# Moving a kernel's SBUF tensors to other offsets from a 64-byte boundary

## The chip, the cores and the metric

The program runs on one core of one Trainium2 chip. The metric is the device time of one launch in microseconds. Three runs of the kernel before gave a median of 2180.43 us, the lowest 2180.04 and the highest 2180.49.

## The reference

Two transformer blocks are computed one behind the other for 512 tokens of width 1024, in float32. The first puts 16 meta tokens ahead (528 tokens); the second works on 512.

```python
def first_block(x, meta_tokens, ...):
    h = concat([meta, x])
    proj = rms_norm(h, g0) @ w_in
    ...
    h = h + rms_norm((sigmoid(g_a) * y_a + sigmoid(g_b) * y_b) @ w_out, g1)
    u = causal_depthwise_conv(rms_norm(h, g2) @ w_up, conv_w, conv_b)
    h = h + rms_norm((gelu(u_gate) * u_val) @ w_down, g3)
    return h[:, N_META:]

def second_block(x, ...):
    h = h + 0.5 * swiglu(rms_norm_2(h, ffn1_norm), ffn1_w_in, ffn1_w_out)
    h = h + hybrid_mixer(...)
    h = h + 0.5 * swiglu(rms_norm_2(h, ffn2_norm), ffn2_w_in, ffn2_w_out)
    h = h + sigmoid(rms_norm_2(h, ple_norm) @ ple_w_gate) * (p @ ple_w_proj)
    return rms_norm_2(h, final_norm)
```

The attention of the first block (forgetting and stick-breaking heads) and the mixer of the second (chunked linear attention and sparse attention) stand in the program too. The bulk of the work is the product of tokens and weight matrices.

## The kernel before, in words

**Weights in units.** All weights come as one stream of units of 128 x 2048 float32 (1 MB each). A unit `u` lands in `raw[u % 2]` (SyncE's queue). ScalarE rounds it to `whi[u % 2]` in one copy of 2048 columns (`weights_hi`, L766 to L771; a few units in pieces, L783 and L793). GpSimd computes `wlo[u % 2] = raw - whi` in pieces of 512 columns, in a few units of 256 or 128 (`low_part`, L702 to L705). SyncE may fill `raw` again when GpSimd is done with it, and ScalarE may write `whi` again when TensorE is through with the unit two before (`unit_done`).

**Three products for one.** The tokens too are kept as a rounded part and a low part: `xhi` and `xlo` in block 1 (8 rows of 528 or 514 tokens, at a stride of 576), `x2hi` and `x2lo` in block 2 (8 rows of 512), `hhi` and `hlo` for the inner rows of the feed-forward layers (22 rows of 512). `tile_products` (L2362 to L2369) takes a weight tile of 128 columns (512 bytes per partition) as the stationary operand and makes three products with it: `whi` with the rounded tokens, `whi` with the low ones, `wlo` with the rounded ones. The tokens are the moving operand:

```python
for p_, (w, xx) in enumerate(((whi, xh), (whi, xl), (wlo, xh))):
    for dst, tok in places:
        ins = mm(dst, w[slot][:, cols], xx(tok), ...)
```

In block 2 one matmul streams 512 tokens. In block 1 a row of 514 or 528 tokens goes as two matmuls, 256 and 258 (or 272). Every matmul has a weight load of its own (an LDWEIGHTS in the trace, engine name PEld). In the trace a matmul is written `ps<-moving,stationary`.

**Places in SBUF.** Everything is placed by hand. `at(name, shape, dtype, offset)` (L223 to L228) puts a tensor at a byte offset in each partition, or at the next free one. The program begins at 16512, and in the kernel before this is how the large ones stand:

| tensor | offset before | modulo 64 | modulo 256 |
|---|---|---|---|
| raw0, raw1 | 16512, 24704 | 0 | 128 |
| whi0, whi1 | 32896, 41088 | 0 | 128 |
| wlo0, wlo1 | 49280, 57472 | 0 | 128 |
| h | 65664 | 0 | 128 |
| xhi (x2hi), xlo | 82560, 100992 | 0 | 128 |
| x2lo | 98944 | 0 | 128 |
| arena (hhi) | 119424 | 0 | 128 |
| hlo | 164480 | 0 | 128 |
| ident | 209536 | 0 | 128 |
| temp | 213408 | 32 | 160 |

"arena" is the shared region: the attention's tensors, the mixer's, `hhi` and `hlo`, the tensors of squares and the output rows all lie in it, nearly all of them at multiples of 64 bytes from its start. "temp" is the scratch region behind the constants, and its tensors start at 32 modulo 64 in the main (`dl`, `dpt`, `sb_lo`, `ntri_r`, `sb_p`, `nt`).

Not everything that TensorE reads starts on the boundary even so. Block 1 leaves the first 14 tokens out from its gates on (`SKIP = 14`): `wide_places(banks, 14)` makes the moving operand start at token 14 of a row, 56 bytes past a boundary, and its second part at token 270, likewise 56 bytes past one. The up projection of block 1 takes rows of 514 tokens from token 0 (`places_of`), on the boundary. `L2592` turns `fox_p` (in arena, on the boundary) with `ident`, and `L3187` turns `dl` (in temp, 32 bytes past one) with `ident`; in both the tile that is turned is the stationary operand. `L3177` streams `dpt` (temp, 32 past) against `ckvt` (arena, 0), `L3104` streams `kx` against `kx` (arena, 0 and 0), and `L2669` streams `sb_hi` (arena, 0) and then `sb_lo` (temp, 32 past) against `ntri_r` (temp, 32 past).

**Order of the work.** Each engine's program is written out by hand, with semaphores between the engines. No planner or scheduler reads the offsets.

Of the kernel before, what the change touches and what calls it, by code (L numbers as in the profile page):

```python
# [25 lines left out]
F32R = mybir.dt.float32r  # L26
# [5 lines left out]
P = 128  # L32
D = 1024
KC = D // P
META = 16
SEQ = 512
# [5 lines left out]
HALF = 256  # L42
XROW = 576
BANK = 512
FF = 2816
FC = FF // P
EPS = 1e-6
NEG = -1e30
UT = 16
# [66 lines left out]
def std_units(w, starts):  # L116

    tiles = w.reshape(KC, P, w.shape[1])
    cut = [tiles[:, :, s:s + P] for s in starts]
    both = [np.stack(cut[i:i + 2]) for i in range(0, len(cut), 2)]  # L120
    return [np.ascontiguousarray(b.transpose(2, 1, 0, 3)).reshape(1, P, UT * P) for b in both]


def row_units(w, start):

    tiles = w[:, start:start + BANK].reshape(2, KC // 2, P, BANK)
    return [np.ascontiguousarray(t.transpose(1, 0, 2)).reshape(1, P, UT * P) for t in tiles]
# [18 lines left out]
def pairs_up(w):  # L146
    starts = []
    for i in range(0, FC, 2):
        starts += [P * i, P * i + P, FF + P * i, FF + P * i + P]
    return std_units(w, starts)  # L150
# [6 lines left out]
def layout(v):  # L157
# [15 lines left out]
    narrow = [w[:, 4112:4240], w[:, 4752:4824], decay, np.zeros((D, 8), np.float32), decay, decay]  # L173
    aw = np.zeros((P, BANK), np.float32)
    stacked = np.zeros((P, 2), np.float32)
# [33 lines left out]
def build(nc, wstream, h0, fw, cvec, alpha_w, rel_bias, p2, ident_c, masks_c, gmask_c, onehot_c, out):  # L209
    n_units = wstream.shape[0]  # L210
    with ExitStack() as ctx:
# [9 lines left out]
        place = {"at": 16512}  # L221

        def at(name, shape, dt=F32, offset=None):  # L223
            size = int(np.prod(shape[1:])) * 4
            if offset is None:
                offset = place["at"]
                place["at"] += (size + 31) // 32 * 32
            return nc.alloc_sbuf_tensor_at(name, list(shape), dt, offset=offset)  # L228

        raw = [at(f"raw{b}", [P, UT * P]) for b in range(2)]  # L230
        whi = [at(f"whi{b}", [P, UT * P], F32R) for b in range(2)]
        wlo = [at(f"wlo{b}", [P, UT * P], F32R) for b in range(2)]
        h = at("h", [P, KC, T1])
        x_at = place["at"]
        xhi, xlo = (at(name, [P, KC, XROW], F32R)[:, :, 0:T1] for name in ("xhi", "xlo"))
        x_spare = x_at + 8 * KC * SEQ
        arena = place["at"]
        place["at"] += 2 * FC * SEQ * 4
        ident = at("ident", [P, P])
        masks_at = place["at"]  # L240
        masks = at("masks", [P, 3 * P + META])
# [21 lines left out]

        ps = ctx.enter_context(nc.psum_tensor("ps", [P, 8 * BANK], F32))
        regions = ps[:].rearrange("p (r c) -> p r c", c=2 * BANK)
        LO = BANK - HALF

# [3 lines left out]
        def bank(i, n=1):  # L271
            return ps[:, i * BANK:(i + n) * BANK]

# [50 lines left out]
        yt = [at(f"yt{i}", [P, TN], offset=temp + 4 * T1 * i) for i in range(4)]  # L324
        mix = at("mix", [P, KC, SEQ], offset=x_at)
        x2hi = at("x2hi", [P, KC, SEQ], F32R, offset=x_at)
        x2lo = at("x2lo", [P, KC, SEQ], F32R, offset=x_at + 4 * KC * SEQ)

        sq = [at(f"sq{i}", [P, T1], offset=temp + 4 * T1 * i) for i in range(2)]
        nt = [at(f"nt{i}", [P, T1], offset=temp + 4 * T1 * (2 + i)) for i in range(3)]  # L330
# [9 lines left out]
            return sq_sum1[:] if T == TN else sq_sum[:, 0:T]  # L340

        hhi = at("hhi", [P, FC, SEQ], F32R, offset=arena)
        hlo = at("hlo", [P, FC, SEQ], F32R, offset=arena + 4 * FC * SEQ)
        cg = at("cg", [P, 2, SEQ], offset=temp)
        gact = at("gact", [P, 2, SEQ], offset=temp + 4096)
        cvl = at("cvl", [P, 2, SEQ], offset=temp + 8224)
# [2961 lines left out]
```

How the kernel before makes its waits and increments, by code:

```python
    def wait(self, value=None):  # L104
        self.eng.wait_ge(self.sem, self.turn + (self.n if value is None else value))
# [571 lines left out]
        @block.sync  # L677
        def _(sp):
            sp.dma_start(cv[:], cvec).then_inc(sig("gains_in"), 16)
            for q in range(4):
                sp.dma_start(h[:, 2 * q:2 * q + 2, :], h0[:, 2 * q:2 * q + 2, :]).then_inc(sig(f"h_in{q}"), 16)
            sp.dma_start(raw[1][:], wstream[1]).then_inc(sig("raw_ready1"), 16)
            with sp.Fori(1, n_units // 2) as i:
                for b in range(2):
                    sp.wait_ge(sig("lo_done"), i * 2 + (b - 1))
                    sp.dma_start(raw[b][:], wstream[bass.ds(i * 2 + b, 1)].rearrange("u p n -> (u p) n")
                                 ).then_inc(sig(f"raw_ready{b}"), 16)
            if n_units % 2:
                sp.wait_ge(sig("lo_done"), n_units - 2)
                sp.dma_start(raw[0][:], wstream[n_units - 1]).then_inc(sig("raw_ready0"), 16)
            for j, half in [(j + e, half) for j in (0, 2) for half in range(2) for e in range(2)]:
                cols = slice(half * BANK, (half + 1) * BANK)
                sp.wait_ge(sig("out_odd" if j % 2 else "out_even"), 2 * (j // 2) + half + 1)
                sp.dma_start(out[0, j * P:(j + 1) * P, cols], outb[j][:, cols]).then_inc(sig("stored"), 16)
            sp.wait_ge(sig("stored"), 128)
# [207 lines left out]
            def fox_hi(m):  # L905
                act.wait_ge(sig("o_done"), m + 2)
                if m == 0:
```

## Time and profile before

| | |
|---|---|
| median of 3 runs | 2180.43 us |
| the profiled execution's own time | 2180.01 us |
| its span in the trace | 2178.2 us |
| TensorE matmuls busy | 2146.8 us (99%), x12490 |
| TensorE weight loads busy | 1851.4 us (85%), x12490 |
| VectorE busy | 995.2 us (46%) |
| ScalarE busy | 755.5 us (35%) |
| GpSimd busy | 1008.7 us (46%) |
| DMA | 195.17 MB, mean 90 GB/s |

The span is the stretch from the first to the last instruction, and the execution's time lies 1.8 us above it. Busy times of an engine are unions of its instructions' spans. Matmuls overlap one another in the trace (each lasts longer than the step from one start to the next), so the pace is read from starts: from a timeline, or from the number of matmuls in a stretch that has no gap.

### The profile page before, as it was taken

The page shows a single profiled execution, that of the slowest core. Times are in us where ns is not written, and L with a number is a line of the kernel's source. Part 1 is how long each engine was busy: PE and PEld are TensorE (multiplying, and loading weights), DVE is VectorE, ACT ScalarE, POOL GpSimd, SP SyncE. Part 2 cuts the span into 40 slices and gives each one's busy share as a digit, 9 for nine tenths or more (in the row PEclk, how much of TensorE's full clock was granted, in tenths as well). Part 3 has the DMA queues.
Part 4 walks back from the last instruction along what each step waited for, and adds up shares of the span by engine and source line. Part 5 has one row for each costly group of instructions (what it writes and reads, how often), then busy time and mean ns, then how long its engine had stood idle before and what let it go on. Part 6 is the DMA issues. An engine that isn't in the chain of part 4 may idle for free.

```text
span 2178.2 us, 31347 instructions
## 1 busy us (share of the span) xinstructions
PE 2146.8 (99%) x12490; PEld 1851.4 (85%) x12490; DVE 995.2 (46%) x1460; ACT 755.5 (35%) x1017; POOL 1008.7 (46%) x825
## 2 busy tenths in 40 slices
PE   8999999999999999999999999999999999999998
PEld 7897999999999887888888788878788888888886
DVE  5144454379888207322200819671876442222027
ACT  4133455243222215322211415551336332222134
POOL 4322223455555547555544545254331555555444
PEclk9999999999999999999999999999999999999999
DMA  4311111212222222322222221114220222222222
GB/s 165 102 69 68 59 48 71 97 59 97 96 83 90 106 96 106 127 96 96 97 97 96 93 109 42 59 58 152 80 78 21 97 97 97 96 96 97 96 100 93
DMA packets 31950, 195.17 MB, mean 90 GB/s; under 512 B 3968, under 2 KB 4480, under 8 KB 10096
## 3 DMA queue, kind: packets, MB, share of 16 engines
q1 hardware_dynamic: 26352, 182.66, 23.1%
q10 hardware_dynamic: 5504, 11.18, 1.6%
q8 instruction: 68, 1.11, 0.2%
q14 instruction: 26, 0.21, 0.0%
HBM read 189.47 MB, written 4.23 MB: 89 GB/s over the span
## 4 chain that ended last, share of the span: by engine, by line
PE 83%; issue 7%; DVE 5%; POOL 3%; ACT 1%; DMA 0%; SPq 0%; DVEq 0%; POOLq 0%; ACTq 0%
PE ps L2367 73%; POOL wlo L705 3%; PE ps L2962 2%; DVE sqa L1517 1%; PE ps L3177 1%; PE ps L3161 1%; PE ps L3044 1%; DVE x2lo L1505 1%; PE ps L3097 1%; PE ps L2646 1%; PE ps L2669 0%; PE ps L3142 0%; PE ps L2705 0%; PE ps L3187 0%; DMA h<-h 0%
## 5 line engine op out<-in xcount | busy, mean ns | idle before, releaser
L705 POOL TENSOR_TENSOR wlo<-raw,whi 128x512 fp32r<-128x512 f32 (+2 forms) x820 | 1007.3, 1261 | 1143.8 <-ACT whi L771 1037.9
L771 ACT CAST whi<-raw 128x2048 fp32r<-128x2048 f32 x162 | 309.6, 1911 | 811.8 <-PE ps L2367 754.5
L2367 PE MATMUL ps<-x2hi,whi 128*128 128x512 f32 x1136 | 448.6, 395 | 1.2 <-DVE x2lo L1505 1.1
L2367 PE MATMUL ps<-x2hi,wlo 128*128 128x512 f32 x1136 | 442.4, 389 | 0.0
L2367 PE MATMUL ps<-x2lo,whi 128*128 128x512 f32 x1136 | 442.1, 389 | 0.0
L2367 PE MATMUL ps<-xhi,whi 128*128 128x256 f32 (+2 forms) x1336 | 273.3, 286 | 11.7 <-DVE xlo L1571 9.3
L2367 PE MATMUL ps<-xlo,whi 128*128 128x256 f32 (+2 forms) x1336 | 270.7, 284 | 0.0
L2367 PE MATMUL ps<-xhi,wlo 128*128 128x256 f32 (+2 forms) x1336 | 270.5, 284 | 0.0
L2367 PEld LDWEIGHTS ps<-x2hi,whi 128*128 128x128 f32 x1136 | 213.3, 188 | 49.7 <-issue 4.8
L2367 PEld LDWEIGHTS ps<-x2hi,wlo 128*128 128x128 f32 x1136 | 213.2, 188 | 44.7
L2367 PEld LDWEIGHTS ps<-x2lo,whi 128*128 128x128 f32 x1136 | 213.4, 188 | 44.4 <-issue 1.7
L2367 PEld LDWEIGHTS ps<-xhi,whi 128*128 128x128 f32 x1336 | 208.6, 191 | 12.9 <-POOL wlo L705 12.0
L2367 PEld LDWEIGHTS ps<-xlo,whi 128*128 128x128 f32 x1336 | 208.7, 191 | 0.0
L2367 PEld LDWEIGHTS ps<-xhi,wlo 128*128 128x128 f32 x1336 | 208.6, 191 | 0.0
L2367 PE MATMUL ps<-hhi,whi 128*128 (+1 forms) x528 | 205.4, 389 | 0.0
L2367 PE MATMUL ps<-hlo,whi 128*128 (+1 forms) x528 | 205.4, 389 | 0.0
L2367 PE MATMUL ps<-hhi,wlo 128*128 (+1 forms) x528 | 205.4, 389 | 0.0
L2367 PEld LDWEIGHTS ps<-hhi,wlo 128*128 128x128 f32 x528 | 99.1, 188 | 20.8
L2367 PEld LDWEIGHTS ps<-hhi,whi 128*128 128x128 f32 x528 | 99.1, 188 | 20.5
L2367 PEld LDWEIGHTS ps<-hlo,whi 128*128 128x128 f32 x528 | 99.1, 188 | 20.4
L1529 DVE TENSOR_TENSOR cvl<-ps,fold 128x1024 f32<-128x1024 f32 x22 | 26.9, 1224 | 189.3 <-PE ps L2367 189.3
L2002 DVE SCALAR_TENSOR_TENSOR h<-ps,h 128x512 f32<-128x512 f32 x16 | 10.9, 681 | 209.7 <-PE ps L2367 209.7
(471 smaller groups left out, 2761.0 us busy)
## 6 DMA issues: line engine op xcount, KB each, us to landing
raw<-wstream SPq DMA_DIRECT2D x170, 1024.0 KB, 4.8
h<-h SPq DMA_DIRECT2D x4, 528.0 KB, 8.5
ncb<-c_rows ACTq DMA_DIRECT2D x8, 256.0 KB, 3.3
ple_rows<-ple_out ACTq DMA_DIRECT2D x4, 512.0 KB, 4.0
bias<-bias_rows ACTq DMA_DIRECT2D x8, 256.0 KB, 4.8
ple<-ple_rows ACTq DMA_DIRECT2D x4, 512.0 KB, 5.4
out_dram<-outb SPq DMA_DIRECT2D x8, 256.0 KB, 2.9
raw<-wstream ACTq DMA_DIRECT2D x4, 256.0 KB, 7.2
```

The lines of the kernel that those rows point to most:

```text
L705: return nc.gpsimd.tensor_tensor(wlo[b][:, cols], raw[b][:, cols], whi[b][:, cols].bitcast(F32), ALU.subtract)
L771: nc.scalar.copy(whi[b][:], raw[b][:]).then_inc(sig("hi_done"), 1)
L1505: vec.scalar_tensor_tensor(out=xl[:, k, 0:T], in0=view(k), scalar=cv[:, gain + k:gain + k + 1], in1=xh[:, k, 0:T].bitcast(F32), op0=ALU.mu ...
L1517: vec.tensor_tensor(squared[:, 0, :], squared[:, 0, :], squared[:, k, :], ALU.add).then_inc(sig("sq_added"), 1)
L1529: return vec.tensor_tensor(dst, pair(src), scale, ALU.mult)
L2367: ins = mm(dst, w[slot][:, cols], xx(tok), start=first and p_ == 0, stop=last and p_ == 2, skip_group_check=True)
L2646: mm(zs[x][:, col + b * P:col + (b + 1) * P], qkb[rows_of(x), 4 + c, b * P:(b + 1) * P], qkb[rows_of(x), c, i * P:(i + 1) * P], start=(q = ...
L2962: ins = mm(gv_bank(half, j), xx[:, k if first else k + 4, tok], ww[u % 2][:, cols], start=(first and k == 0 and p_ == 0), stop=(not first ...
L3044: ins = mm(bank(5 + e)[:, t_ * P:(t_ + 1) * P], gvt[:, s_, (2 * hd + e) * P:(2 * hd + e + 1) * P], rhs, start=(x_ == 0), stop=(x_ == len(p ...
L3097: ins = mm(dst, left, right, start=True, stop=True)
L3161: mm(dst, dq[:, hd, j * P:(j + 1) * P], ckvf[:, 0:w], start=True, stop=False)
L3177: ins = mm(bank(6 + m % 2)[:, 0:P], ckvt[:, b, :], dpt[m % 2][:, b * P:(b + 1) * P], start=(b == 0), stop=(b == j))
```

## The change

Four things are moved; no instruction is added, removed or put elsewhere. `raw` stays where it is, and so do the order and the shape of every matmul, copy and transfer.

```diff
+SKEW = (0, 32, 64, 128)
...
-        whi = [at(f"whi{b}", [P, UT * P], F32R) for b in range(2)]
-        wlo = [at(f"wlo{b}", [P, UT * P], F32R) for b in range(2)]
+        w_at = place["at"]
+        whi, wlo = ([at(name + str(b), [P, UT * P], F32R, offset=w_at + (2 * i + b) * 4 * UT * P + SKEW[2 * i + b])
+                     for b in range(2)] for i, name in enumerate(("whi", "wlo")))
+        place["at"] = w_at + 4 * (4 * UT * P) + 128
         h = at("h", [P, KC, T1])
         x_at = place["at"]
         xhi, xlo = (at(name, [P, KC, XROW], F32R)[:, :, 0:T1] for name in ("xhi", "xlo"))
-        x_spare = x_at + 8 * KC * SEQ
-        arena = place["at"]
-        place["at"] += 2 * FC * SEQ * 4
+        x_spare = x_at + 8 * KC * SEQ + 32
+        arena = place["at"] + 32
+        place["at"] += 32 + 2 * FC * SEQ * 4 + 32
...
-        x2lo = at("x2lo", [P, KC, SEQ], F32R, offset=x_at + 4 * KC * SEQ)
+        x2lo = at("x2lo", [P, KC * SEQ + 8], F32R, offset=x_at + 4 * KC * SEQ)[:, 4:4 + KC * SEQ].rearrange(
+            "p (k n) -> p k n", n=SEQ)
...
-        hlo = at("hlo", [P, FC, SEQ], F32R, offset=arena + 4 * FC * SEQ)
+        hlo = at("hlo", [P, FC * SEQ + 8], F32R, offset=arena + 4 * FC * SEQ)[:, 4:4 + FC * SEQ].rearrange(
+            "p (k n) -> p k n", n=SEQ)
```

Where the tensors stand with it:

| tensor | offset after | modulo 64, before -> after | modulo 256 after |
|---|---|---|---|
| raw0, raw1 | 16512, 24704 | 0 -> 0 | 128 |
| whi0 | 32896 | 0 -> 0 | 128 |
| whi1 | 41120 | 0 -> 32 | 160 |
| wlo0 | 49344 | 0 -> 0 | 192 |
| wlo1 | 57600 | 0 -> 0 | 0 |
| h | 65792 | 0 -> 0 | 0 |
| xhi (x2hi), xlo | 82688, 101120 | 0 -> 0 | 0 |
| x2lo | 99088 | 0 -> 16 | 16 |
| arena (hhi) | 119584 | 0 -> 32 | 32 |
| hlo | 164656 | 0 -> 48 | 48 |
| ident | 209728 | 0 -> 0 | 64 |
| temp | 213600 | 32 -> 32 | 96 |

## Rows read from the trace of the kernel before

**Rows 1.** The page: busy time, share and instructions of TensorE's matmuls and loads.

```profile
PE 2146.8 (99%) x12490; PEld 1851.4 (85%) x12490; DVE 995.2 (46%) x1460; ACT 755.5 (35%) x1017; POOL 1008.7 (46%) x825
```

**Rows 2.** The page's costliest groups: busy us, mean ns, then idle before and its releaser.

```profile
L2367 PE MATMUL ps<-x2hi,whi 128*128 128x512 f32 x1136 | 448.6, 395 | 1.2 <-DVE x2lo L1505 1.1
L2367 PE MATMUL ps<-x2lo,whi 128*128 128x512 f32 x1136 | 442.1, 389 | 0.0
...
L2367 PE MATMUL ps<-xhi,whi 128*128 128x256 f32 (+2 forms) x1336 | 273.3, 286 | 11.7 <-DVE xlo L1571 9.3
...
L2367 PEld LDWEIGHTS ps<-x2hi,whi 128*128 128x128 f32 x1136 | 213.3, 188 | 49.7 <-issue 4.8
...
L2367 PE MATMUL ps<-hhi,whi 128*128 (+1 forms) x528 | 205.4, 389 | 0.0
L2367 PE MATMUL ps<-hlo,whi 128*128 (+1 forms) x528 | 205.4, 389 | 0.0
```

**Rows 3.** Busy time by stretch: block 2's up projection, down projection, block 1's up projection.

```profile
core 0: us, PE busy (x) PEld busy (x) DVE busy (x) ACT busy (x) POOL busy (x), PEclk, DMA share, GB/s
900.00:1050.00 150.00, 150.00 (x664) 124.20 (x663) 40.40 (x28) 40.85 (x28) 78.48 (x56) 1.00 0.26 97
1100.00:1160.00 60.00, 60.00 (x267) 49.67 (x266) 0.00 (x0) 9.54 (x5) 29.30 (x24) 1.00 0.24 89
500.00:650.00 150.00, 150.00 (x1250) 149.80 (x1249) 132.24 (x115) 38.78 (x27) 82.24 (x53) 1.00 0.25 91
```

**Rows 4.** Timeline of TensorE, block 1, moving operand from token 0: start us, length us.

```profile
600.08 0.40 PE L2367 MATMUL ps<-xhi,wlo 128*128 128x256 f32 x2
...
601.28 0.28 PE L2367 MATMUL ps<-xlo,whi 128*128 128x256 f32 x1
```

**Rows 5.** Timeline of TensorE, block 1, moving operand from token 14.

```profile
218.55 0.40 PE L2367 MATMUL ps<-xlo,whi 128*128 128x256 f32 x2
...
220.71 0.28 PE L2367 MATMUL ps<-xlo,whi 128*128 128x256 f32 x1
```

**Rows 6.** Lines L2592, L3187, L3177 and L3104: duration ns min/median/max.

```profile
L2592 PEld LDWEIGHTS ps<-ident,fox_p x80: 138/141/144, 111.8 to 232.6; 128*128 128x128 f32 x80
L2592 PE MATMUL ps<-ident,fox_p x80: 272/273/328, 111.9 to 232.7; 128*128 128x128 f32 x80
...
L3187 PEld LDWEIGHTS ps<-ident,dl x80: 137/141/146, 1624.9 to 1671.0; 128*128 128x128 f32 x80
L3187 PE MATMUL ps<-ident,dl x80: 272/273/332, 1625.2 to 1671.1; 128*128 128x128 f32 x80
...
L3177 PE MATMUL ps<-dpt,ckvt x160: 270/275/347, 1627.1 to 1672.3; 128*128 128x128 f32 x160
...
L3104 PE MATMUL ps<-kx,kx x16: 275/275/275, 1344.4 to 1403.4; 128*128 128x128 f32 x16
```

**Rows 7.** Groups of TensorE by shape: the matmul with both operands 32 past.

```profile
L2669 PE MATMUL ps<-sb_lo,ntri_r 128*128 128x512 f32 x20 | 7.9, 394 | 0.0
```

**Rows 8.** Timeline of GpSimd, block 2's up projection; in brackets its idle time before.

```profile
957.71 6.32 POOL L705 TENSOR_TENSOR wlo<-raw,whi 128x512 fp32r<-128x512 f32 x4 [5.89 <-ACT whi L771]
968.53 5.04 POOL L705 TENSOR_TENSOR wlo<-raw,whi 128x512 fp32r<-128x512 f32 x4 [4.50 <-ACT whi L771]
```

**Rows 9.** Line L771, duration as above, and groups of ScalarE by shape.

```profile
L771 ACT CAST whi<-raw x162: 1888/1912/1941, 15.6 to 2142.7; 128x2048 fp32r<-128x2048 f32 x162
...
L1001 ACT CAST sb_hi<-sb_p 128x512 fp32r<-128x512 f32 x20 | 12.1, 623 | 9.4 <-DVE sb_p L1778 9.4
L783 ACT CAST whi<-raw 128x512 fp32r<-128x512 f32 x20 | 11.9, 607 | 0.0
```

## The prediction
> **What bounds the kernel now.** I read the page first. TensorE's matmuls cover 2146.8 us of a span of 2178.2 [rows 1], so all idle time of TensorE together is 31.4 us. VectorE, ScalarE and GpSimd are busy for less than half of the span. So the kernel can get shorter or longer by more than a per cent only if the step from one matmul to the next changes, or if another engine gets so much slower that TensorE has to wait for it.
>
> The costliest groups came next [rows 2]. Nearly all of TensorE's time lies in one line, L2367, the three products. Block 2 has 1136 matmuls of each of three kinds with 512 moving columns, the three feed-forward down projections 528 of each of three kinds, block 1 three times 1336 of some 257 columns. Their mean durations (389 ns, 286 ns) are no pace, since they overlap. The pace comes from stretches without a gap [rows 3]: 664 matmuls touch 150 us of block 2's up projection, two of which only reach over the edges, so 150 us / 662 = 226.6 ns a step. The down projection gives 60 us / 265 = 226.4 ns, block 1's up projection 150 us / 1248 = 120.2 ns. The granted clock in all three is 1.00 [rows 3], the upper level of 2.4 GHz. At that clock 512 columns take 213.3 ns and 257 take 107.1 ns. So each step holds 13.3 ns or 13.1 ns beside the stream, and these are about the same for a long stream and for one of half the length. Only this rest could be a matter of where operands lie: 4992 x 13.3 ns + 4008 x 13.1 ns = 66.4 + 52.5 = 119 us. The question is whether it is one.
>
> **The change part by part.** Nothing is added or taken out. Of the offsets modulo 64, `whi0`, `wlo0` and `wlo1` do not move at all (their shifts of 0, 64 and 128 bytes are whole multiples of 64), nor do `raw`, `h`, `xhi`, `xlo`, `x2hi`, `ident` and temp. What moves is `whi1` (to 32), `x2lo` (16), `hhi` and everything else in arena (32) and `hlo` (48). I cost four things.
>
> (a) *Moving operands off the boundary*: `x2lo` in 1136 matmuls, `hhi` and `hlo` in 3 x 528 = 1584, together 2720. The trace of before has the same product with a moving operand on the boundary and off it. On it, in block 1's up projection, five pairs of matmuls (256 and 258 columns) take 601.28 - 600.08 = 1.20 us, 240 ns a pair [rows 4]. At token 14, 56 bytes past the boundary in both parts of the pair, nine pairs take 220.71 - 218.55 = 2.16 us, again 240 ns [rows 5]. The difference is nothing, and the timeline's last digit (0.01 us over nine pairs) leaves 1.1 ns a pair, 0.6 ns a matmul, in either direction. A stream of 512 columns crosses twice as many boundaries, so I allow 1.2 ns: 2720 x 1.2 ns = 3.3 us, up or down. I take 0, since both pairs read 240.
>
> This is weighed against a rule. By the Trainium skill ("SBUF — State Buffer", Door 1, on cachelines) an access that crosses into a new line of 16 bytes costs a penalty. All new offsets are multiples of 16, so by that rule none of the moved operands touches a line more, and the term is 0; rows 5, whose start lies 8 bytes past such a line, show no cost even there.
>
> (b) *Stationary operands off the boundary*: loads from `whi1`. It serves every second unit and two of three products, about a third of 12490 loads. The trace has the same load on and off the boundary: `fox_p` lies at 0, `dl` at 32 modulo 64, each is turned with `ident` in 80 matmuls, and their loads last 138/141/144 ns and 137/141/146 ns, their matmuls 272/273 ns both [rows 6]. In block 2 a load lasts 188 ns of a step of 226.6 [rows 2, 3], so 38 ns more would be hidden. In block 1 the loads cover 149.80 of 150 us [rows 3] and could be what sets the step. There a change by the last digit of these durations, 1 ns, on a third of 4008 loads would be 1.3 us. I take 0.
>
> (c) *ScalarE and GpSimd on moved tiles.* The rows give one hint of a price: ScalarE's copy of 512 columns takes 607 ns from a source on the boundary and 623 ns from one 32 bytes past it [rows 9], though the two also differ in what they wait for. Taken at its worst that is 16 ns for 512 columns, 64 ns on the 1912 ns of a unit of `whi1` [rows 9]. No row shows GpSimd with other offsets. What hides both: TensorE works 48 x 226.6 ns = 10.9 us on a unit, and the next unit needs 1.9 us on ScalarE and then 5.0 to 6.3 us on GpSimd [rows 8, 9], 8.2 us at most. So 2.7 us are free, over 40% of GpSimd's work; its idle time of 4.50 and 5.89 us before a unit [rows 8] says the same. Cost 0. If GpSimd took over 40% longer, TensorE would wait at each unit.
>
> (d) *What is on the path between the stages.* All waits of TensorE together are 31.4 us [rows 1]. If every operation that ends one were longer in the proportion 623 to 607 [rows 9], that would be 31.4 x 0.026 = 0.8 us. I take 0 here too.
>
> **Sum.** The profiled execution took 2180.0 us with its span of 2178.2 and 1.8 us around it, and lies 0.4 us under the median of the runs, 2180.4. The change adds 0, with bounds of -3.3 us and +3.3 + 1.3 + 0.8 = +5.4 us. So I forecast **2180.4 us**, with 2177.1 to 2185.8 as this case's own bounds. A measurement of this kernel can tell 0.2%, some 4.4 us, from no change.
>
> **Rivals.**
>
> *The clash goes (faster).* The rest of 13.3 ns a step may be a clash inside SBUF: the stream and the next tile's load read from the same offset modulo 64 at the same time. For it: in before all large operands share the offset 0, and the rest is the same in every group. Where the moving operand is moved, 2720 matmuls, the clash would go: 2720 x 13.3 ns = 36.2 us, **2144.2 us**. It decides from 1.6 ns a matmul (4.4 us / 2720). Against it: rows 5 have moving and stationary operands 56 bytes apart and run at the same 240 ns as rows 4, where they share the offset. A chance of 9%, for offsets like 16 and 48 that no row has, and for lesser gains.
> A page has the same gain from another side. By the Trainium skill ("TensorE: Matmul & The Clock Gate", Back-to-back issue gap) matmuls of 512 columns follow each other in N/2.4 + 2.5 ns, 215.8 ns; by that the trace is 10.8 ns over, and the moved 2720 would give 29.4 us if the offset were the reason. The same page (LDWEIGHTS, Part 2) gives TensorE two independent read ports, for stream and loads, and by that there is no clash to lose.
>
> *Each stream off the boundary pays (slower).* The one matmul of 512 columns with both operands 32 bytes past the boundary, `sb_lo` against `ntri_r`, lasts 394 ns on average [rows 7], against 389 ns for the dense products [rows 2]. If these 5 ns are the price of an offset, it falls on the 2720 matmuls of `x2lo`, `hhi` and `hlo`, in the feed-forward layers and in the mixer's projections: 2720 x 5 ns = 13.6 us, **2194.0 us**. It too decides from 1.6 ns a matmul. Against it: only 20 matmuls, between neighbours of other shapes, which change a modelled end; and rows 4 and 5 again. A chance of 14%, which includes a GpSimd that takes over 40% longer on `whi1`.
>
> *The change does less than it says.* Three of the four shifts of the weight buffers are multiples of 64, so for them nothing could come even if the offset modulo 64 mattered. It gives the forecast's time and is part of its chance.
>
> **How the numbers follow.** No change has 77%, since the two rows that could have shown an effect, one for each operand, show none to within a nanosecond. The faster rival has 9%, the slower one 14%. The range must take in a bit more than the likeliest case: it goes from 2176.5, just under its lower bound, to 2187.0, half the price of the slower rival (2180.4 + 6.8). Left out are the full prices of both rivals.
>
> **What would show it.** Right: `x2lo` and `hlo` products keep 389 ns, 150 us of block 2's up projection hold 664 matmuls or one or two more or fewer, and the down projection's 60 us hold 267; loads from `whi` keep 188 ns; the idle time of TensorE stays near 31 us. The faster rival would show as some 677 matmuls in those 150 us (three steps of 226.6 ns less 13.3) and 283 in those 60; the slower one as some 659 and 261. Steps that differ between odd and even units would tell of `whi1`. New waits of TensorE for GpSimd's L705 at every second unit would say that (c) was wrong. The forecast is wrong if 16 or 48 bytes act otherwise than the 32 and 56 that the rows hold.

## The result and the profile after

The changed kernel is slower: 2212.1 us (median of four runs, 2211.92 to 2212.38), against 2180.2 us for the kernel before on the same chip, a ratio of 1.0147 with a 95% interval from 1.0135 to 1.0159. The forecast was no change, 2180.4 us, in a range from 2176.5 to 2187.0.

The page of the changed kernel, busy time and the groups that answer to those of [rows 2] (L2367 is now L2372):

```profile
span 2210.2 us, 31347 instructions
...
PE 2179.2 (99%) x12490; PEld 1852.8 (84%) x12490; DVE 992.5 (45%) x1460; ACT 756.6 (34%) x1017; POOL 1006.8 (46%) x825
...
L2372 PE MATMUL ps<-x2hi,whi 128*128 128x512 f32 x1136 | 453.9, 400 | 0.8 <-DVE x2lo L1510 0.7
L2372 PE MATMUL ps<-x2hi,wlo 128*128 128x512 f32 x1136 | 449.6, 396 | 0.0
L2372 PE MATMUL ps<-x2lo,whi 128*128 128x512 f32 x1136 | 447.0, 393 | 0.0
L2372 PE MATMUL ps<-xhi,whi 128*128 128x256 f32 (+2 forms) x1336 | 272.7, 285 | 12.6 <-DVE xlo L1576 9.4
...
L2372 PEld LDWEIGHTS ps<-x2hi,whi 128*128 128x128 f32 x1136 | 213.5, 188 | 54.2 <-issue 4.6
...
L2372 PE MATMUL ps<-hhi,wlo 128*128 (+1 forms) x528 | 208.3, 395 | 0.0
L2372 PE MATMUL ps<-hhi,whi 128*128 (+1 forms) x528 | 208.2, 394 | 0.0
L2372 PE MATMUL ps<-hlo,whi 128*128 (+1 forms) x528 | 207.4, 393 | 0.0
```

The number of instructions is the same, and so are the busy times of the other engines to 3 us. TensorE's idle time is 31.0 us (2210.2 - 2179.2), as before (31.4). No wait has come in: the whole loss of 32.0 us in the span is in the matmuls themselves. Every product with 512 columns got longer, by 4 to 7 ns, **also those whose moving operand did not move modulo 64** (`x2hi` with `whi` and `wlo`). The products with 256 to 272 columns and the weight loads kept their means to 1 ns.

The three stretches of [rows 3] in the changed kernel, same columns:

```profile
900.00:1050.00 150.00, 150.00 (x647) 120.99 (x646) 37.66 (x26) 37.91 (x26) 77.65 (x55) 1.00 0.26 91
1100.00:1160.00 60.00, 60.00 (x260) 48.57 (x259) 2.05 (x1) 10.37 (x6) 30.71 (x24) 1.00 0.25 88
500.00:650.00 150.00, 150.00 (x1247) 150.00 (x1246) 131.54 (x115) 38.86 (x27) 81.58 (x53) 1.00 0.26 91
```

With two matmuls over the edges left out, the step in block 2 is 150 us / 645 = 232.6 ns (226.6 before), in the down projection 60 / 258 = 232.6 (226.4), in block 1's up projection 150 / 1245 = 120.5 (120.2). The granted clock is 1.00 in all three, so it has no part in it. The loss adds up step by step: both kernels have the same 12490 matmuls in the same order, so each step from one start to the next can be compared with its like before. The steps of the x2 products grew by 19.1 us in all, those of `hhi` and `hlo` by 8.7, the other products with 512 columns (three sets of 192 in the mixer with other moving tokens, two of 192 with the weights as the moving operand) by 4.4, block 1's by 0.7; steps over 320 ns, which hold the waits, shrank by 1.0. That is 31.9 us.

The timeline of TensorE in the changed kernel, block 2's up projection, start and length in us; between the two rows lie nine rounds of three products:

```profile
900.09 0.39 PE L2372 MATMUL ps<-x2hi,whi 128*128 128x512 f32 x1
...
906.39 0.39 PE L2372 MATMUL ps<-x2hi,whi 128*128 128x512 f32 x1
```

A round takes 6.30 us / 9 = 700 ns, where before it took 680 (three times 226.7). The single steps from start to start in such a round are 229, 234 and 237 ns in one unit, and go through a cycle of nine values between 225 and 238 ns in the next (mean 231.9); before, all were 226 or 227. So the units of both weight buffers are slowed, and not only those of `whi1`.

### The profile page after: what moved, and what is told of

Same layout as the page of the kernel before. It is cut to its first block, busy times and chain, and to the rows that moved or that the text cites. A ratio compares the mean times of both kernels' runs of the same rounds, so it can differ in the third digit from the quotient of the medians.

```text
span 2210.2 us, 31347 instructions
## 1 busy us (share of the span) xinstructions
PE 2179.2 (99%) x12490; PEld 1852.8 (84%) x12490; DVE 992.5 (45%) x1460; ACT 756.6 (34%) x1017; POOL 1006.8 (46%) x825
## 4 chain that ended last, share of the span: by engine, by line
PE 85%; issue 7%; DVE 4%; POOL 3%; ACT 1%; DMA 0%; SPq 0%; DVEq 0%; POOLq 0%; ACTq 0%
PE ps L2372 75%; POOL wlo L710 3%; PE ps L2967 2%; PE ps L3182 1%; PE ps L3166 1%; PE ps L3049 1%; PE ps L3102 1%; PE ps L2651 0%; PE ps L2674 0%; PE ps L3147 0%; PE ps L2710 0%; PE ps L3192 0%; DMA h<-h 0%; DVE sqa L1522 0%; DVE h L1566 0%
## 5 line engine op out<-in xcount | busy, mean ns | idle before, releaser
L710 POOL TENSOR_TENSOR wlo<-raw,whi 128x512 fp32r<-128x512 f32 (+2 forms) x820 | 1005.5, 1259 | 1176.7 <-ACT whi L776 1070.0
L776 ACT CAST whi<-raw 128x2048 fp32r<-128x2048 f32 x162 | 309.6, 1911 | 840.0 <-PE ps L2372 781.5
L2372 PE MATMUL ps<-x2hi,whi 128*128 128x512 f32 x1136 | 453.9, 400 | 0.8 <-DVE x2lo L1510 0.7
L2372 PE MATMUL ps<-x2hi,wlo 128*128 128x512 f32 x1136 | 449.6, 396 | 0.0
L2372 PE MATMUL ps<-x2lo,whi 128*128 128x512 f32 x1136 | 447.0, 393 | 0.0
L2372 PE MATMUL ps<-xhi,whi 128*128 128x256 f32 (+2 forms) x1336 | 272.7, 285 | 12.6 <-DVE xlo L1576 9.4
L2372 PE MATMUL ps<-xhi,wlo 128*128 128x256 f32 (+2 forms) x1336 | 271.4, 285 | 0.0
L2372 PE MATMUL ps<-xlo,whi 128*128 128x256 f32 (+2 forms) x1336 | 270.3, 284 | 0.0
L2372 PEld LDWEIGHTS ps<-x2hi,whi 128*128 128x128 f32 x1136 | 213.5, 188 | 54.2 <-issue 4.6
L2372 PEld LDWEIGHTS ps<-x2lo,whi 128*128 128x128 f32 x1136 | 213.4, 188 | 52.3 <-issue 1.7
L2372 PEld LDWEIGHTS ps<-x2hi,wlo 128*128 128x128 f32 x1136 | 213.2, 188 | 50.6
L2372 PEld LDWEIGHTS ps<-xhi,whi 128*128 128x128 f32 x1336 | 208.5, 190 | 13.8 <-POOL wlo L710 13.1
L2372 PE MATMUL ps<-hhi,wlo 128*128 (+1 forms) x528 | 208.3, 395 | 0.0
L2372 PEld LDWEIGHTS ps<-xhi,wlo 128*128 128x128 f32 x1336 | 208.3, 190 | 0.0
L2372 PE MATMUL ps<-hhi,whi 128*128 (+1 forms) x528 | 208.2, 394 | 0.0
L2372 PEld LDWEIGHTS ps<-xlo,whi 128*128 128x128 f32 x1336 | 208.0, 190 | 0.0
L2372 PE MATMUL ps<-hlo,whi 128*128 (+1 forms) x528 | 207.4, 393 | 0.0
L2372 PEld LDWEIGHTS ps<-hhi,wlo 128*128 128x128 f32 x528 | 99.0, 188 | 23.7
L2372 PEld LDWEIGHTS ps<-hlo,whi 128*128 128x128 f32 x528 | 99.2, 188 | 23.5
L2372 PEld LDWEIGHTS ps<-hhi,whi 128*128 128x128 f32 x528 | 99.3, 188 | 22.9
```

What stands on the lines that cost most here:

```text
L710: return nc.gpsimd.tensor_tensor(wlo[b][:, cols], raw[b][:, cols], whi[b][:, cols].bitcast(F32), ALU.subtract)
L776: nc.scalar.copy(whi[b][:], raw[b][:]).then_inc(sig("hi_done"), 1)
L2372: ins = mm(dst, w[slot][:, cols], xx(tok), start=first and p_ == 0, stop=last and p_ == 2, skip_group_check=True)
```

## The experiments

Two questions: does the 64-byte boundary of an operand count (theory A), or the place of the operands against each other (theory R; the first four expectations call it theory B)? And with what period, and in which direction? The kernel before gives a hint that the prediction overlooked: all large operands of it stand not just on 64-byte boundaries but at the same place modulo 512 (32896, 82560, 98944, 119424 and 164480 all leave 128). "Distance" below is a token operand's offset minus that of the weight tiles. It is given modulo 512, which is the length of a weight tile; the length of a block 2 token row, 2048 bytes, is a multiple of it. Block 1's rows have a stride of 2304 bytes, so there the distance of a row alternates between the one given and 256 bytes more.

Every kernel of this section but the last was run once. The kernel before, in 15 runs, lay between 2179.9 and 2180.8 us, so differences of 12 us and more are far outside its spread. The first four stand beside one run of it at 2179.9 us.

**weights_only.** The weights as in the change, the rest back.

```diff
-        place["at"] = w_at + 4 * (4 * UT * P) + 128
+        place["at"] = w_at + 4 * (4 * UT * P) + 256
...
-        x_spare = x_at + 8 * KC * SEQ + 32
-        arena = place["at"] + 32
+        x_spare = x_at + 8 * KC * SEQ
+        arena = place["at"]
```
(`x2lo` and `hlo` have no shift of their own; all that stands behind the weights is 256 bytes further than in the kernel before)

> The four weight buffers stand as in the changed kernel (whi1 32 bytes past a 64-byte boundary, wlo0 and wlo1 shifted by 64 and 128); x2lo, hhi, hlo and the shared region are back on multiples of 256 bytes from where they stood before. Theory A (each operand off a 64-byte boundary pays by itself, and 2720 moving operands carry most of it): most of the 32 us goes, about 2185 us, and in block 2's up projection only the unit in whi1 has steps above 226.6 ns. Theory B (what counts is where the moving stream lies relative to the load that runs beside it, and before all were alike): the offsets between stream and loads are still changed, so the steps stay near 232 ns in units of both buffers and the time near 2205 to 2212 us. Theory C (placement modulo 128 or 256 bytes counts): as B here.

Measured: 2202.8 us.

**tokens_only.** `SKEW = (0, 0, 0, 0)` and no gap behind the weights; the token side as in the change.

> The weight buffers stand as before; x2lo (+16), the shared region with hhi (+32) and hlo (+48) as in the changed kernel. Theory A: nearly the whole loss, some 2205 us; x2hi steps stay at 226.6 ns and those of x2lo, hhi and hlo grow by 5 to 15 ns. Theory B: a loss as well, but also in steps of x2hi beside which no load has moved only if the order of phases drifts; between 2195 and 2212 us. Both expect the same for odd and even units, since the two buffers are alike again.

Measured: 2206.6 us. Either half of the change alone has most of the whole loss, 23 and 27 of 32 us, so the two halves do not add up.

**all_by_64.** `SKEW = (0, 64, 64, 128)`, shared region and `x2lo` each 64 bytes further.

> Every shift is a multiple of 64 bytes: weights 0, 64, 64, 128, x2lo +64, shared region +64. Theory A and a theory B that counts modulo 64: the time of before, 2180 us, all steps 226.6 ns. Theory C (the offsets modulo 128 or 256 bytes count): a loss of 10 us or more, with steps that differ from 226.6 ns.

Measured: 2212.6 us, the changed kernel's time with every large tensor back on a 64-byte boundary. Theory A falls here.

**low_parts_only.** `x2lo` and `hlo` 16 bytes off, the rest at multiples of 64 bytes from its old place (the shared region at 256).

> Only x2lo and hlo are 16 bytes off; everything else is at multiples of 256 bytes from its place before. Theory A: 1136 + 528 = 1664 matmuls pay, 10 to 20 us, in their own step alone. Theory B: a loss of like size; the step of x2lo or hlo changes and its neighbours may too. If the low parts cost nothing: 2180 us.

Measured: 2205.4 us. The groups of block 2's up projection (900 to 1050 us) show that the products whose operands stand as before pay too. First the kernel before, then this one:

```profile
L2367 PE MATMUL ps<-x2hi,whi 128*128 128x512 f32 x222 | 86.4, 389 | 0.0
L2367 PE MATMUL ps<-x2lo,whi 128*128 128x512 f32 x221 | 86.0, 389 | 0.0
L2367 PE MATMUL ps<-x2hi,wlo 128*128 128x512 f32 x221 | 86.0, 389 | 0.0
```

```profile
L2373 PE MATMUL ps<-x2hi,wlo 128*128 128x512 f32 x216 | 85.5, 396 | 0.0
L2373 PE MATMUL ps<-x2lo,whi 128*128 128x512 f32 x216 | 85.1, 394 | 0.0
L2373 PE MATMUL ps<-x2hi,whi 128*128 128x512 f32 x216 | 84.9, 393 | 0.0
```

The mixer's products with 512 columns whose operands all moved by 256 bytes or not at all (`xr`, `gy`, `my`, 571 steps compared) stayed the same to 0.2 ns a step on average.

**tokens_by_32, tokens_by_64, tokens_by_256.** The whole token side moved as one against the weights, which stand as before.

```diff
-        x_at = place["at"]
+        x_at = place["at"] + 32
+        place["at"] += 32
```

> All token operands (xhi, xlo, x2hi, x2lo, and the shared region with hhi and hlo) are moved together by 32 bytes against the weight buffers, and keep their places relative to each other. Before, every large operand stood at the same place modulo 512 bytes. Theory S (all streams, and all loads, must be alike among themselves): they still are, so 2180 us and steps of 226.6 ns. Theory R (what counts is the distance of the stream from the load beside it): the distance is now 32 for every pair, so all steps of a unit are alike but another value than 226.6, up or down, and both buffers show it; 5 ns a step would be 30 us. Theory A (each operand off a 64-byte boundary): 226.6 ns plus a price in every step.

> The same with 64 bytes. Theory S: 2180 us. Theory R: another value than 226.6 ns in every step, near that of 32 bytes if the effect is smooth. Theory A: 2180 us, since nothing is off a 64-byte boundary.

> The same with 256 bytes. Theory S: 2180 us. Theory R: if the pattern repeats in 256 bytes or less, 226.6 ns and 2180 us; if in 512 (a weight tile is 512 bytes wide, a token row 2048), this is the largest distance there is, and the steps are other than 226.6 ns, by the sum of the first runs some 230 to 235 ns and 2205 to 2215 us, or below 226.6 if the equal places of before are the worst.

Measured, beside 2180.7 us for the kernel before: 2211.7, 2193.1 and 2181.2 us. Block 2's up projection, the stretch 900 to 1050 us of each, in this order:

```profile
900.00:1050.00 150.00, 150.00 (x645) 120.47 (x644) 37.22 (x27) 39.29 (x27) 73.31 (x53) 1.00 0.27 98
```
```profile
900.00:1050.00 150.00, 150.00 (x657) 123.05 (x657) 38.33 (x27) 40.67 (x28) 76.08 (x54) 1.00 0.27 98
```
```profile
900.00:1050.00 150.00, 150.00 (x663) 124.21 (x662) 40.39 (x28) 40.84 (x28) 77.73 (x55) 1.00 0.27 98
```

Steps of 233.3, 229.0 and 226.9 ns. Theory S, that streams need only be alike among themselves, is out: they are alike here, and 32 bytes cost 31 us. 64 bytes, which leave every operand on its boundary, cost 12 us; 256 bytes cost 0.5 us in one run, less than the 0.9 us by which the runs of the kernel before differ. These are means of a round. At 64 bytes the three products of a round have steps of 232 (`x2hi,whi`), 226 (`x2lo,whi`) and 229 ns (`x2hi,wlo`), though all three have the same distance: the distance sets the mean, not each single step.

**dist_16_128_16, dist_48_96_192, dist_96_16_128, dist_8_8_48.** One distance for each set of token operands in one kernel: `xhi`/`xlo` (inside their rows, which have 192 bytes to spare), `x2hi`/`x2lo`, `hhi`/`hlo`. For the first:

```diff
-        xhi, xlo = (at(name, [P, KC, XROW], F32R)[:, :, 0:T1] for name in ("xhi", "xlo"))
+        xhi, xlo = (at(name, [P, KC, XROW], F32R)[:, :, 4:4 + T1] for name in ("xhi", "xlo"))
...
-        x2hi = at("x2hi", [P, KC, SEQ], F32R, offset=x_at)
+        x2hi = at("x2hi", [P, KC * SEQ + 32], F32R, offset=x_at)[:, 32:32 + KC * SEQ].rearrange(
+            "p (k n) -> p k n", n=SEQ)
```
(likewise `x2lo`, `mix` and the small tensors in their place, `hhi` and `hlo`)

> All weight buffers as before. Each pair of token operands (rounded and low part alike) has a distance of its own from the weight tiles: xhi/xlo 16 bytes, x2hi/x2lo 128, hhi/hlo 16 (528). Theory R (a step depends on this distance alone): each group has one mean step of its own; so far 32 bytes gave 233.3 ns, 64 gave 228.9, 256 and 0 gave 226.7. I expect hhi/hlo at 16 above 228 ns, x2 at 128 between 226.7 and 229, falling towards the period. Theory A (each operand's own 64-byte boundary): x2 226.7, hhi/hlo at 233. If the cost grows with the row's place in the region rather than with the distance, none of this holds and groups that share a distance differ.

> The same with 48 bytes for xhi/xlo, 96 for x2hi/x2lo, 192 for hhi/hlo. Theory R with a period of 64 bytes would give 96 the 233.3 ns of 32, which theory A gives as well; with a period of 256 the distance of 192 equals -64 and should be as 64 or mirrored, up to 229 ns. A step below 226.6 ns anywhere would make a faster kernel.

> The same with 96, 16 and 128 bytes. Theory R: x2 at 16 and hhi/hlo at 128 repeat, to 0.3 ns, the means that hhi/hlo at 16 and x2 at 128 have in the kernel before this one. If they do not, the distance alone is not the cause.

> The same with 8, 8 and 48 bytes (560). Theory R, where the unit is a line of 16 bytes: 8 bytes cost little or nothing; where the unit is 64 bytes, 8 and 48 lie with 32 at 230 ns or more. In block 1, where 32 bytes gave 120.1 ns for 121.4, distances under 64 should give some of the same gain.

Measured, beside 2180.2 us: 2202.4, 2212.0, 2209.3 and 2209.7 us. Mean step of TensorE by distance, worked out from the starts in each trace (all steps of the group under 260 ns; block 1 is its up projection, 500 to 700 us, steps under 150 ns of 256 and 258 columns):

| distance, bytes | x2 products, ns | hhi/hlo products, ns | block 1, ns |
|---|---|---|---|
| 0 (before) | 227.0 | 226.7 | 120.0 |
| 8 | 233.0 | | 120.0 |
| 16 | 231.7 | 231.7 | 117.5 |
| 32 | 233.3 | 233.3 | 118.3 |
| 48 | | 233.3 | 116.7 |
| 64 | 229.0 | 228.9 | 118.3 |
| 96 | 233.4 | | 118.9 |
| 128 | 232.9 | 233.0 | |
| 192 | | 233.3 | |
| 256 | 227.0 | 226.7 | 120.0 |

A distance gives the same mean step to two sets of operands in different regions: to 0.1 ns at 16 and 128 (in different kernels), 32 and 64, and to 0.3 ns at 0 and 256. The cost is neither smooth nor mirrored: 64 costs 2.2 ns, 192 costs 6.7. Nothing tried is under 226.7 ns for 512 columns, so the kernel before stood at the best place found, and the slowest step is 233.3 to 233.4 ns: 6.7 ns more, which at 2.4 GHz is the time of 16 columns. The expected repeat of 16 and 128 in the third kernel came, within the 0.3 ns asked for. My expectation that 128 lies near the minimum, between 226.7 and 229, missed; so did those that 192 costs as much as 64, that 8 bytes might cost little, and that every distance under 64 gives block 1 some gain (8 gives none).

Block 1 goes the other way: 0, 8 and 256 are the worst distances of the table. Its streams from token 14 (200 to 350 us) lie 56 bytes further on; there the kernel before (56 bytes) has 120.0 ns, dist_8_8_48 (64) 118.5 and tokens_by_64 (120) 121.0, so block 1 has slower places too. Down projection of the first and the third kernel, for `hhi`/`hlo` at 16 and at 128 (one matmul more or less in 260 is 0.9 ns a step, so these counts are coarser than the table):

```profile
1100.00:1160.00 60.00, 60.00 (x260) 48.70 (x260) 0.00 (x0) 11.45 (x6) 25.91 (x21) 1.00 0.30 105
```
```profile
1100.00:1160.00 60.00, 60.00 (x259) 48.27 (x258) 1.68 (x1) 9.55 (x5) 29.27 (x23) 1.00 0.26 89
```

**together_by_32.** Weights, tokens and shared region all 32 bytes further: `SKEW = (32, 32, 32, 32)`, 32 bytes behind the weights.

> Weight buffers, tokens and shared region all 32 bytes further, so every operand of the large products is off a 64-byte boundary and every distance is 0. Theory R (the distance between stream and weight tiles, modulo 256 bytes, sets the step): 226.7 ns a step for 512 columns and 2180 us, as before. Theory A (an operand's own boundary): 233 ns as with the tokens alone moved by 32 bytes, 2212 us.

Measured: 2181.1 us, beside 2180.5. Every operand of the large products is off its 64-byte boundary, and the stretch of block 2 is that of [rows 3] to one matmul:

```profile
900.00:1050.00 150.00, 150.00 (x663) 124.20 (x662) 40.34 (x28) 40.80 (x28) 77.99 (x55) 1.00 0.28 98
```

So with 512 columns an operand's own boundary costs nothing that these runs can tell, and the distance between tokens and weights carries the loss. `raw` stayed where it was, so the place of tokens and weights against `raw` does not count either.

**wlo_by_32.** Only `wlo0` and `wlo1` moved: `SKEW = (0, 0, 32, 32)`, 256 bytes behind the weights.

> Only wlo0 and wlo1 are moved, by 32 bytes. If a stream is slowed by the load that runs beside it: in block 2's up projection the x2lo product (beside it, wlo is loaded) is slow, some 235 ns or more, and the other two stay near 226.7. If by its distance from its own stationary tile: the x2hi,wlo product is slow. Either way less than the 31 us that all three cost at 32 bytes; a third would be some 10 us, 2190 us, but the patterns of the first runs say that a phase drifts on from one step to the next, so all three may move and the sum may be up to 2205 us.

Measured: 2215.5 us, the slowest of all, where at most 2205 was expected. The groups of block 2's up projection:

```profile
L2373 PE MATMUL ps<-x2lo,whi 128*128 128x512 f32 x215 | 86.0, 400 | 0.0
L2373 PE MATMUL ps<-x2hi,whi 128*128 128x512 f32 x215 | 84.9, 395 | 0.0
L2373 PE MATMUL ps<-x2hi,wlo 128*128 128x512 f32 x215 | 83.6, 389 | 0.0
```

The product that is made with the moved `wlo` kept its 389 ns. The longest is `x2lo,whi`, beside which the moved tile is loaded. That is what a stream held up by the load beside it would show, and not what its own stationary tile would. But `x2hi,whi`, beside which an unmoved tile is loaded, has 395, and the steps from start to start (232 ns for `x2hi,whi`, 239 for `x2lo,whi`, 229 for `x2hi,wlo`) are all over 226.7. So moving one tile changes all steps of a round, and the run does not settle which operands are in each other's way. It does speak against GpSimd, which writes the moved `wlo`: all 214 steps of `x2lo,whi` in the 150 us are 239 ns, while GpSimd is busy for 77.63 of them.

**xhi_by_16.** The version that the table points to: block 2 stays at distance 0, block 1 gets 16. The whole edit to the kernel before:

```diff
-        xhi, xlo = (at(name, [P, KC, XROW], F32R)[:, :, 0:T1] for name in ("xhi", "xlo"))
+        xhi, xlo = (at(name, [P, KC, XROW], F32R)[:, :, 4:4 + T1] for name in ("xhi", "xlo"))
```

> Only xhi and xlo of block 1 are moved, by 16 bytes inside their rows; block 2 keeps its distance of 0. From the stretches of the kernel that had 16 bytes there: 2.5 us less in block 1's up projection, 0.9 in its output projection, some 1.1 in the stretches with attention. Theory R: 2175.5 us, 0.2% less than before. If gains in block 1 are given back as waits for VectorE (88% busy in the up projection) or at the start of block 2: 2178 to 2180.

Measured: 2176.0 us (median of 11 runs) against 2180.5 (15 runs), a ratio of 0.9981, interval 0.9972 to 0.9990. It beats both kernels. Its stretches of block 1 and block 2:

```profile
500.00:650.00 150.00, 148.23 (x1262) 148.03 (x1261) 134.20 (x116) 38.72 (x27) 81.52 (x52) 1.00 0.27 92
900.00:1050.00 150.00, 150.00 (x664) 124.20 (x663) 39.58 (x28) 38.52 (x28) 78.70 (x56) 1.00 0.26 94
```

Between 480 and 710 us TensorE now has a wait that it had not before:

```profile
PE ps L2367 <- POOL wlo L705: 1.8, 1, 1.8
```

Block 2 is unchanged at 664. Block 1's up projection has 2112 products (22 units of 96); at 2.5 ns less each (120.0 to 117.5) they should give 5.3 us. Not all of it is kept: only 12 more matmuls fit into the 150 us, since 1.77 us of them are idle now (150 - 148.23). TensorE waits there, by the profile for GpSimd; GpSimd got its unit from ScalarE, which rounded it (from 541.13 us) right behind a cast of `hhi` for which it had waited 5.15 us for VectorE. A second new wait of 1.7 us, for VectorE (`first_up`, L1869), lies at 476 us. Compared step by step with the kernel before, all `xhi` and `xlo` products of block 1 take 8.7 us less, and 3.8 us of that are given back as idle time. The whole kernel gained 4.5 us, near the 5 expected. At 48 bytes, with 116.7 ns a step, the idle part is larger still (147.82 us busy of the same 150, in dist_48_96_192), which is why 16 bytes were taken; 48 bytes in block 1 alone were not run.

## Why the prediction was wrong

**What bounds the kernel** was right: only the step of the matmul could move the time, and it did. The rest of 13.3 ns a step was rightly named as the only part that placement could touch, and it grew to 19 ns.

**Term (a) is the step that failed.** It took the cost of a moving operand off the boundary as 0, "since both pairs read 240" in [rows 4] and [rows 5], and widened that to 512 columns. Three things were wrong with it.
- It looked at a boundary, where the distance counts. together_by_32 has every large operand off the boundary at no cost, all_by_64 has none off it and costs 33 us.
- So it counted 2720 matmuls. In truth all products with 512 columns pay, the 2272 of `x2hi` too: in the changed kernel `x2hi` stands 128 and 96 bytes from `whi0` and `whi1` and 64 and 0 from `wlo0` and `wlo1`, where before all four distances were 0.
- The rows are of block 1. There the step depends on the distance in another way than in block 2: 0 and 8 bytes read 120.0 ns and 16 bytes read 117.5, while block 2 has 226.7, 233.0 and 231.7 ns. Two points of such a curve that happen to be equal (0 and 56 bytes) were taken for a flat line, and the timeline's last digit for its uncertainty.

**Term (b)**, loads, failed too, for the same reason. The loads' durations did stay (188 ns in block 2; in block 1 the loads cover 150.00 of 150 us, 149.80 before). But comparing L2592 with L3187 [rows 6] could not show the effect. Those streams have 128 columns at a moving operand of their own, and it is not a load's length that the distance changes but the step from one matmul to the next. weights_only moved the weights against everything else and cost 23 us, where this term had 0 to 1.3.

**Terms (c) and (d)** were right. ScalarE's copies took 1911 ns on average in both kernels, GpSimd's pieces 1259 ns after and 1261 before, and TensorE's idle time stayed at 31 us. One slip in the range: 2180.4 + 6.8 is 2187.2 and not 2187.0, which changes nothing here.

**The rivals.** The slower one had the sign and nearly the size of a step (5 ns; measured 6.0 in the up projection), read off the `sb_lo` row [rows 7]. It had the wrong place, 2720 matmuls in place of all that stream 512 columns, and so 2194.0 us in place of 2212.1. Its sign for the down projection, 261 matmuls, fits the 260 found, and the one for the up projection, 659, does not (647), since it gave `x2hi` no price. Its row, a matmul between neighbours of other shapes, was no proof of the mechanism it named; that the 5 ns came near was luck. The faster rival had the right kind of cause, the place of the stream against that of the loads, with the sign turned round: it held equal offsets for the worst case, and in block 2 they are the best one found. In block 1 it was right for 16 bytes, as xhi_by_16 shows; 8 bytes, also unequal, gain nothing there. The third rival, that three of four shifts are multiples of 64 and do nothing, fell with all_by_64 and tokens_by_64 (12 us for 64 bytes).

**The rule of the Trainium skill** ("SBUF — State Buffer", Door 1) on lines of 16 bytes, in term (a), gave 0 as well, and the time does not follow it: low_parts_only moves two operands by exactly 16 bytes, so their streams touch no line more, and costs 25 us. In block 1 a start 8 bytes past a line costs nothing either (dist_8_8_48, 120.0 ns as at 0). The gap of 2.5 ns above N/2.4 that the Trainium skill ("TensorE: Matmul & The Clock Gate", Back-to-back issue gap) gives for a matmul by itself, without the loads, is not reached at any distance tried: the least is 13.3 ns above the stream with 512 columns, and 9.6 ns with 257 (116.7 ns at 48 bytes, where 257 columns take 107.1). The two independent read ports that the Trainium skill gives TensorE (same page, Part 2) cannot be the whole account here, since moving the loaded tiles alone makes the steps longer (wlo_by_32, weights_only).

**Still open.** Why the distance counts at all: that accesses of stream and loads clash is a guess that no run shows. Nor is it known why 64 bytes cost less than 32 or 192. Mean steps lie between 226.7 and 233.4 ns, as if up to 16 columns' time were added to 32; why they end there was not tried. That the pattern repeats after 256 bytes rests on 0 and 256 alone. Products without a load of their own, distances between those listed and a distance of its own for the attention outputs of block 1 were not tried.

## What to carry to other kernels

Where TensorE is the bound and each matmul has its own weight load, as here, the place of the moving operand against the stationary tiles is a parameter of the kernel like any other: here it is worth 3% of a step with 512 columns and as much, at other distances, with 256. Read it from the steps between starts in a steady stretch, and scan it with several operand sets at different distances in one run; in this kernel a pad that shifts the tokens by 32 bytes against the weights costs 31 us with nothing else changed. And two equal points are no flat line: before a price is set to zero from a comparison, it wants a third point, in the same shape as the work it is used for.

## What was not expected of the hardware

- The mean step of a product with 512 columns depends on the distance between token operand and weight tile: 226.7 to 227.0 ns at 0 and 256 bytes, 228.9 at 64, 231.7 at 16, 232.9 to 233.4 at 8, 32, 48, 96, 128 and 192.
- With 256 and 258 columns it is 120.0 ns at 0, 8 and 256 bytes, and 116.7 to 118.9 at 16 to 96.
- Where only some operands are moved, the steps of the others grow too: 32 bytes on `wlo` alone cost 35 us, more than 32 bytes on all tokens (31 us).
- An operand's own 64-byte boundary made no difference: 2181.1 us with the large ones off it, 2180.5 with them on it.
